# Loading most of the third query chunk ahead of the expert gathers, and giving the gathers other buffers

## What is computed

```
def peer(h, w_query, sub_keys, expert_u, expert_v):
    ...
    def block(xb):
        q = (xb @ w_query).reshape(PEER_BLOCK, PEER_HEADS, 2, PEER_QDIM // 2)
        s = jnp.einsum('thpd,hpnd->thpn', q, sub_keys)
        sv, si = lax.top_k(s, PEER_TOPK)
        cand = (sv[:, :, 0, :, None] + sv[:, :, 1, None, :]).reshape(...)
        ...
        top_s, pos = lax.top_k(cand, PEER_TOPK)
        idx = jnp.take_along_axis(cidx, pos, axis=-1)
        gate = jax.nn.softmax(top_s.astype(jnp.float32), axis=-1)
        act = jax.nn.gelu(jnp.einsum('thkd,td->thk', expert_u[idx], xb).astype(jnp.float32))
        return jnp.einsum('thk,thkd->td', (gate * act).astype(xb.dtype), expert_v[idx])
```

## Time and profile before

| | |
|---|---|
| median of 3 runs | 1901.68 us (1900.18 to 1902.64) |
| the profiled execution | 1899.87 us |
| its span, first to last instruction | 1898.1 us |
| granted TensorE clock over the span | 0.986 |
| busy: TensorE, VectorE, ScalarE, GpSimd | 84%, 57%, 21%, 38% of the span |
| read from HBM | 720.57 MB |

### The profile page before, as it was taken

The page is one execution under the profiler, slowest core; times in us unless marked ns, Lnnn a source line. Parts: engine busy times, 40 slices in busy tenths (PEclk is TensorE's granted clock), DMA queues, the critical chain, the costliest instruction groups (busy, mean ns, idle before and its releaser), DMA issues.

```text
span 1898.1 us, 13797 instructions
## 1 busy us (share of the span) xinstructions
PE 1595.1 (84%) x4603; PEld 758.1 (40%) x4603; DVE 1086.1 (57%) x1801; ACT 393.9 (21%) x1154; POOL 727.2 (38%) x574
## 2 busy tenths in 40 slices
PE   4999999999999959999977877777777777777776
PEld 1446444556458844443323322222222223222332
DVE  1137896675768784432546646465574655646444
ACT  2001003223011012222212222121231212222112
POOL 0010010001104365555655455554646546555441
PEclk7999999999999989999999999999999999999999
DMA  9999776739987999999999999999999999999997
GB/s 369 387 342 345 285 291 233 271 140 358 371 293 300 412 422 423 422 423 422 423 423 422 422 422 422 422 423 422 422 423 422 422 423 422 423 422 422 423 422 294
DMA packets 147736, 723.63 MB, mean 381 GB/s; under 512 B 10889, under 2 KB 13289, under 8 KB 81106
## 3 DMA queue, kind: packets, MB, share of 16 engines
q0 software_dynamic: 92800, 612.73, 78.6%
q1 hardware_dynamic: 52208, 107.30, 15.4%
q10 hardware_dynamic: 2658, 2.72, 0.6%
HBM read 720.57 MB, written 2.14 MB: 381 GB/s over the span
## 4 chain that ended last, share of the span: by engine, by line
DMA 45%; PE 43%; DVE 5%; POOL 4%; issue 2%; SPq 1%; ACT 1%; DVEq 0%; ACTq 0%
DMA ring<-in_expert_v,acc 17%; DMA H<-in_expert_v,acc 14%; PE ps L995 12%; PE ps L1286 11%; DMA ring<-in_expert_u,acc 7%; PE ps L1130 6%; PE ps L917 3%; PE ps L1245 3%; DMA modrow<-in_expert_v,acc 3%; POOL ring L463 2%; DMA gwork<-in_expert_u,acc 2%; DMA qh<-in_expert_u,acc 2%; PE ps L1186 1%; PE ps L991 1%; PE ps L882 1%
## 5 line engine op out<-in xcount | busy, mean ns | idle before, releaser
L1286 PE MATMUL ps<-ring,wg 128*128 128x512 f32 x1168 | 533.0, 602 | 157.9 <-DMA ring<-in_expert_v,acc 157.9
L1757 DVE SCALAR_TENSOR_TENSOR ring<-ring,A 128x2048 f32<-128x2048 f32 x135 | 308.3, 2291 | 308.2 <-DMA ring<-in_expert_u,acc 308.0
L1286 PEld LDWEIGHTS ps<-ring,wg 128*128 128x128 f32 x1168 | 213.8, 191 | 474.9 <-issue 293.4
L1286 PE MATMUL ps<-H,wg 128*128 128x512 f32 x576 | 263.4, 602 | 64.9 <-DMA H<-in_expert_v,acc 64.9
L463 POOL DMA_INDIRECT ring<-in_expert_v,acc x146 | 199.9, 1369 | 236.3 <-PE ps L1286 225.0
L797 ACT ACTIVATE wg<-K,VX 128x128 f32<-128x128 f32 x256 | 102.8, 402 | 670.8 <-PE ps L1286 669.3
L995 PE MATMUL ps<-ring,H 128*128 128x512 f32 x512 | 222.2, 594 | 1.2 <-ACT VX L594 1.2
L463 POOL DMA_INDIRECT ring<-in_expert_u,acc x135 | 173.4, 1284 | 92.4 <-issue 41.7
L1286 PEld LDWEIGHTS ps<-H,wg 128*128 128x128 f32 x576 | 105.5, 191 | 221.1 <-issue 131.1
L1319 DVE SCALAR_TENSOR_TENSOR acc<-ring,vec,acc 128x512 f32<-128x512 f32 x240 | 180.4, 752 | 21.9 <-DMA ring<-in_w_mod 13.5
L1286 PE MATMUL ps<-modrow,wg 128*128 128x512 f32 x288 | 131.7, 600 | 36.7 <-DMA modrow<-in_expert_v,acc 36.7
(11 more groups left out here) (285 smaller groups left out, 1404.5 us busy)
## 6 DMA issues: line engine op xcount, KB each, us to landing
ring<-in_w_mod POOLq DMA_DIRECT2D x32, 2048.0 KB, 10.4
ring<-in_w_mod SPq DMA_DIRECT2D x32, 1024.0 KB, 14.4
ring<-in_w_in SPq DMA_DIRECT2D x14, 2048.0 KB, 13.2
ring<-in_w_query SPq DMA_DIRECT2D x8, 2048.0 KB, 18.2
ring<-in_w_out SPq DMA_DIRECT2D x12, 1024.0 KB, 12.3
ring<-in_expert_v,acc POOLq DMA_INDIRECT x150, 28.8
ring<-in_expert_u,acc POOLq DMA_INDIRECT x135
B<-in_ctx SPq DMA_DIRECT2D x2, 1024.0 KB, 14.8
```

The source lines that it names most:

```text
L1286: ins = mm(ps[:, 4 * b + n, :], diag[:, r % 4, :], v_rows[r % V_SLOTS][:, n * CH:(n + 1) * CH], start=k == 0, stop=r == BLOCK_RANKS - 1, s ...
L1757: v.scalar_tensor_tensor(out=rows_u, in0=rows_u, scalar=1.0, in1=A[:, r // BLOCK_RANKS, :], op0=ALU.mult, op1=ALU.mult, accum_out=dots[:, ...
```

## The change

The third chunk (n = 2) no longer goes into `W[2]` and `W[3]` as a whole. Its half kh = 1 is loaded in two quarters into `KT` and `gwork`, the second quarter of kh = 0 into `gy`, all three behind chunk 0 in SyncE's order; only the first quarter of kh = 0 still goes into `W[2]`, where it waits for `w_free` 42. TensorE takes the weights from these four places and waits for their semaphores. As `KT`, `gwork` and `gy` (slots 8, 6, 7) are taken until `w_free` 45 and 46, the first U ranks get the slots 4, 9, 10, then rows 6, 7 and 5 of `ring` (slots 2, 3, 1), for which GpSimd waits for `w_free` 41 and 42. Slots 8, 6, 7 and 0 come first in `MIDDLE_SLOTS`, and `LATE_SLOTS` is (6, 0, 2, 3, 1, 4, 5).

```
@@ -53,9 +53,9 @@
 SPREAD_ORDER = (0, 1, 2, 3)
 RANKS = TB * PH * TOPK
 BLOCK_RANKS = PH * TOPK
-EARLY_SLOTS = (4, 7, 8, 6, 9, 10) + (4, 7, 8, 6) * 3 + (4, 7)
-MIDDLE_SLOTS = (2, 3, 0, 1, 4, 7, 8, 6)
-LATE_SLOTS = (2, 3, 0, 1, 4, 6, 5)
+EARLY_SLOTS = (4, 9, 10, 4, 2, 3, 1) + (4, 2, 3, 1) * 3 + (4,)
+MIDDLE_SLOTS = (8, 6, 7, 0, 2, 3, 1, 4)
+LATE_SLOTS = (6, 0, 2, 3, 1, 4, 5)
 FIRST_SLOTS = EARLY_SLOTS + 2 * MIDDLE_SLOTS
 LEAD = 40
 FIRST_V = 9
@@ -247,6 +247,8 @@
                   qh[:].rearrange("p a b t -> p (a b t)"), gwork[:], gy[:], KTf[:, 0:D],
                   Hf[:, 4096:6144], Hf[:, 6144:8192]]
         v_rows = [*(ring[:, i, :] for i in range(4)), Hf[:, 0:D], Hf[:, D:2 * D], modrow[:]]
+        fours = lambda row: row.rearrange("p (k n) -> p k n", k=4)
+        WQ2 = {1: [KT[:], fours(gwork[:])], 0: [W[2][:, 0:4], fours(gy[:])]}
         diag = wgf[:, 0:4 * P].rearrange("p (s n) -> p s n", s=4)
 
         mb = qh[:].rearrange("p a b t -> p (a b t)").rearrange("p (s d t) -> p s d t", s=4, d=2)
@@ -255,7 +257,7 @@
 
 
         names = """ym_ready first_picked picked top_ready pick_step ld_id ld_const ld_dft ld_c ld_rows ld_x0 ld_x1 ld_ctx0 ld_ctx1 ld_wg ld_bg ld_gy ld_bm
-        ld_x2 ld_gffn st_mod ld_ga1 ld_sc2 ld_sh2 rows_psum rows_spread ld_keys ld_gfin bg_zero silu_c vec_psum vec_ready vecz_zero vecz_ready moda_free
+        ld_x2 ld_gffn st_mod ld_ga1 ld_sc2 ld_sh2 rows_psum rows_spread ld_keys ld_wq2 ld_gfin bg_zero silu_c vec_psum vec_ready vecz_zero vecz_ready moda_free
         modcol_psum mod_ready ssq std rstd xn_ready xT_psum ht_act ht_dve w_free m_free row_sum
         row_free proj_free gate_parts_psum gate_parts_ready gates_psum abs_ready ln_ready thr_in st_neg thr_ready u_ready uT_psum
         uT_ready kconv qconv k_ready q_ready ones_v fn1_done fn1_free fn2_done fn2_free s_done
@@ -356,6 +358,11 @@
                     k0 = (kh * KH + 4 * i) * P
                     sp.dma_start(WO[piece % 3][i], w_out[0][k0:k0 + 4 * P, n * CH:(n + 1) * CH].rearrange(
                         "(k p) n -> p k n", p=P)).then_inc(o_ld[piece % 3], 16)
+            def load_third_query(kh, i, loaded):
+                k0 = (kh * KH + 4 * i) * P
+                sp.dma_start(WQ2[kh][i], w_query[0][k0:k0 + 4 * P, 2 * CH:3 * CH].rearrange(
+                    "(k p) n -> p k n", p=P)).then_inc(loaded, 16)
+
             def load_query(n, kh):
                 base, loaded = (2, q_ld) if n % 2 == 0 else (0, w_ld)
                 sp.dma_start(W[base + kh], w_query[0][kh * KH * P:(kh + 1) * KH * P,
@@ -365,10 +372,20 @@
             for kh in range(2):
                 sp.wait_ge(S["m_free"], 2 * (MODB - 1) + kh + 1)
                 load_query(0, kh)
+            sp.wait_ge(S["w_free"], 38)
+            for i in range(2):
+                load_third_query(1, i, S["ld_wq2"])
+            sp.wait_ge(S["keys_psum"], 16)
+            load_third_query(0, 1, early_ld[3])
             for n in range(1, 4):
                 for i, kh in enumerate(HALVES):
+                    if n == 2 and kh == 1:
+                        continue
                     sp.wait_ge(S["w_free"], 36 + 2 * n + i + 1)
-                    load_query(n, kh)
+                    if n == 2:
+                        load_third_query(0, 0, q_ld[0])
+                    else:
+                        load_query(n, kh)
             sp.wait_ge(S["pair_free"], RANKS - 2)
             for n in range(4):
                 sp.wait_ge(S["final_ready"], n + 1)
@@ -481,6 +498,10 @@
             pool.wait_ge(S["first_picked"], 1)
             gather(expert_u[0], u_rows[u_slot(0)], 0, u_ld[u_slot(0)], first_idx)
             for r in range(1, LEAD):
+                if r == EARLY_SLOTS.index(2):
+                    pool.wait_ge(S["w_free"], 41)
+                if r == EARLY_SLOTS.index(1):
+                    pool.wait_ge(S["w_free"], 42)
                 if r == len(EARLY_SLOTS):
                     pool.wait_ge(S["w_free"], 45)
                 if r == len(EARLY_SLOTS) + 2:
@@ -1233,17 +1254,20 @@
                 if n == 3:
                     pe.wait_ge(S["q_free"], 2)
                 for part, kh in enumerate(HALVES):
-                    if n == 2:
+                    if n == 2 and kh == 1:
+                        pe.wait_ge(S["ld_wq2"], 32)
+                    elif n == 2:
+                        pe.wait_ge(early_ld[3], 64)
                         pe.wait_ge(q_ld[kh], 32)
                     else:
                         pe.wait_ge(w_ld[kh], 16 * (8 + n // 2))
-                    wq = W[(2 if n == 2 else 0) + kh]
+                    wq = WQ2[kh] if n == 2 else halves_of(W[kh])
                     for j in range(4):
                         for k in range(KH):
                             kk = kh * KH + k
 
                             ins = mm(ps[:, 2 * (n % 2) + j // 2, (j % 2) * T:(j % 2 + 1) * T],
-                                     wq[:, k, j * P:(j + 1) * P], h2T[:, kk, :],
+                                     wq[k // 4][:, k % 4, j * P:(j + 1) * P], h2T[:, kk, :],
                                      start=part == 0 and k == 0 and j % 2 == 0,
                                      stop=part == 1 and k == KH - 1, skip_group_check=True)
                     ins.then_inc(S["w_free"], 1)
```

## The result

The changed kernel took 1909.99 us (median of 6 runs, 1909.65 to 1914.29) against 1901.18 us for the kernel before beside it (6 runs, 1899.09 to 1903.35): a ratio of 1.005, interval 1.0037 to 1.0063. It is 8.8 us slower; the prediction's sum was 1909.6.

What follows compares the result with a forecast made beforehand. The prediction took the 16 transfer engines, full from 590 us on, as the bound. Early loads and early gaps cost nothing, the 7.45 us saved were swallowed, V0 came 7.9 us later: 1901.68 + 7.9 = 1909.6 us, range 1905 to 1913.

Steps and rivals of the forecast that it cites:

- Early loads: SyncE's three quarter loads behind chunk 0: 3.15 MB fit into room before the first gather at 579.31, cost nothing.
- Three-buffer start: First U ranks on fewer buffers: gaps of a few us around 603 and ahead of 658, costed at nothing.
- cover: VectorE's wait ahead of norm_soft: dot 31 ends at 688.5, norm_soft starts at 694.09, so 5.6 us cover the early gaps.
- the 7.45 us: Full transfer stretch from 590: 7.45 us shorter with 3 MiB of loads gone, a saving swallowed by the gap before V0.
- The deciding term: GpSimd's ranks 38 and 39 wait for dots 32 and 33, behind norm_soft and pick(3) on VectorE: V0 7.9 us later.
- V0: First V gather, needed at 710.17 before; forecast to go out at 710.8 and be ready at 718.1, 7.9 us later.
- the way from there to V0: From rank 38's issue at 707.3: 5.85 us through an empty stream, then rank 39 and V0 one transfer each, 718.1.
- The faster rival: Stream never runs dry, ranks 38 and 39 do not hold GpSimd: V0 6.6 us earlier, 1895.1 us; chance 0.09.
- the holes at 600 and 650: Gaps of a few us in the gather stream around 603 and again ahead of 658, costed at nothing.
- the late wait: GpSimd held at rank 38 until dot 32 ends at 707.03 on VectorE, with all nine opening V gathers behind rank 39.

Runs made afterwards that it cites:

- e8: Changed kernel with the dots of ranks 32 and 33 put ahead of norm_soft and pick(3) on VectorE; 1901.17 us, ratio 1.0005 to the kernel before.
- e6: Changed kernel with the dots of ranks 33 to 47 on 8 columns only, VectorE nearly idle behind dot 32; 1909.03 us, ratio 1.0048 to before.
- e5: Changed kernel with dots 32 to 47 as two instructions of 1024 columns each; 1909.34 us, ratio 1.0046 to the kernel before.
- e7: Changed kernel with each dot of ranks 32 to 47 as four instructions of 512 columns; 1909.25 us, a single run.
- e4_both: Changed kernel with ranks 36 to 39 on slots of ranks 28 to 31 and MIDDLE_SLOTS taking slots 7 and 0 last; 1896.7 us, ratio 0.9978 to before.
- e1: Changed kernel with ranks 36 to 39 given the slots of ranks 28 to 31, as before the change; 1902.65 us, ratio 1.0008 to before.

## Why the prediction was right, and where it was off

**Early loads, costed at 0: right.** SyncE's timeline after (two halves of chunk 0, the quarters into `KT`, `gwork` and `gy`):

```profile
544.94 6.67 SPq L368 DMA_DIRECT2D ring<-in_w_query  x2
551.65 0.58 SPq L363 DMA_DIRECT2D KT<-in_w_query  x1
552.27 0.51 SPq L363 DMA_DIRECT2D gwork<-in_w_query  x1
553.16 2.91 SPq L363 DMA_DIRECT2D gy<-in_w_query  x1
```

544.94 + 6.67 - 3.9 = 547.7, as written. Queries and chunk 3 kept their times. The rate in this stretch shows that the bytes went where there was room.

**Three-buffer start, costed at 0: right here, with less cover than written; the 7.45 us were not to be had.** norm_soft starts at 697.99 - 3.9 = 694.09, to the hundredth. The cover was thinner than I had worked out: dot 31 ends at 695.45 - 3.9 = 691.55, not 688.5, and 2.53 us of VectorE's idleness are left instead of 5.6. The gather of rank 22 took 668.97 - 661.87 = 7.1 us to its dot instead of 5.85, and from dot 22 to dot 31 they stand (693.16 - 668.97) / 9 = 2.69 us apart instead of 2.485. What was wrong is the term beside it, a full stretch 7.45 us shorter. Up to 660 no gather moved up (22.02 MB before and in e8), so what the loads left free stood empty. The start itself made ranks 6 to 9 about 4 us later, but rank 10 goes out at 610.97 in e8 and at 610.24 before. e8 shows the sum: nothing won.

**The deciding term: right in cause, mis-sized by 2 us.** "V0 comes 7.9 us later" was +10.0. Dot 32 ended at 710.83 - 3.9 = 706.93 (forecast 707.03) and rank 38 went out at 707.5 (707.3). The step that was off is the way from there to V0: 10.8 forecast, 12.67 measured. Of the 1.9 us, 1.2 are issues held by dots (e6). The other 0.65 is a remainder without a test of its own: three gathers into an empty stream take that much longer than one of 5.85 and two of 2.485. I had priced an issue by the earlier trace rows where VectorE was at norm_soft and pick(3). A hint at a longer one stood in the earlier trace rows: GpSimd's busy time is 54.21 / 33 = 1.64 us per issue while dots run, and 10.52 / 11 = 0.96 from 690 to 710. That the total came out closer (+8.8 against +7.9) is in part luck: the medians moved 1.2 us less than V0, while the span of the profiled execution, less the shift, grew by 10.5.

The Trainium skill's page "SBUF — State Buffer", section "SBUF: two separate sides", says that GpSimd and VectorE share a port pair that one of them holds for a whole instruction, and that a VectorE operation with two SBUF inputs holds it against GpSimd work that reads SBUF. A dot has two such inputs, and e6's 0.93 against 1.91 us agrees; whether an issue is work that reads SBUF, no run here shows. That VectorE's whole instruction shuts an issue out does not explain e5, where an issue takes two half dots, nor e7, whose quarters have two inputs as well and delay the V gathers by nothing.

**The faster rival, 1895.1: mispriced.** It left ranks 38 and 39 out of the count. Behind rank 37 at 701.1 come three gathers, not one: 701.1 + 3 x 2.485 = 708.6, a gain of 1.6, not 6.6. The rest of the 7.45 fell into the holes at 600 and 650, which I had named and costed at nothing. e8, which is this rival made real, gave 1901.17. The verdict didn't hang on it; but without the late wait the change would have ended within 0.2% of before, and not at 1895.1.

**Bytes tell much the same.** From 555 to 730 us (shifted as above) the windows' rates give, beside the span of the profiled execution (less the shift, against 1898.1) and the median time:

| kernel | 555 to 579 | 579 to 730 | MB against before | at 422 GB/s | span | time |
|---|---|---|---|---|---|---|
| before | 176 GB/s | 402 GB/s | | | | |
| the change | 298 | 350 | 24 x 0.122 - 151 x 0.052 = -4.92 | +11.7 us | +10.5 | +8.8 |
| e8_dots_first | 298 | 378 | -0.70 | +1.7 | +0.6 | +0.3 |
| e4_both | 300 | 392 | +1.47 | -3.5 | -3.7 | -4.1 |

The change brings 2.9 MB forward and loses 7.9 MB behind. e8 brings back 4.2 of these, e4 2.1 more. The bytes meet the spans to 1.2 us.

## What to carry to other kernels

Where transfers bound a kernel, a transfer moved into idle time wins only if the transfers behind it can move up and no later issue comes late: list, for every gather that gets another buffer, which instruction frees that buffer and what stands ahead of it on its engine. One gather that waits holds every transfer written behind it on its queue. Moving two dots, or choosing the next slots by when they come free, was worth 7 to 13 us here; the loads that were moved could bring 7.45 at most.

## Not expected of the hardware

A gather's issue on GpSimd took 0.93 us with VectorE idle, 1.91 to 2.47 us beside whole dots of 2.29 us (2048 columns, two SBUF inputs), 1.40 to 1.99 us beside half dots of 1.15, and for V gathers 0.94 us again beside quarters of 0.61. Behind a full queue this costs nothing (e4 issues every 2.2 us and moves 420 GB/s); after a hole, as in e1, the issues stand further apart than a gather takes to pass. The wait also left TensorE idle for 28.41 us, and its granted clock from 724 to 728, when it worked again, was 0.50, the 1.2 GHz level; from V0 to the end it is 1188.4 us, against 1187.9 before, so no cost of that clock can be told.
